# Residual tails and the products behind them, each made in two halves of 256 tokens

## The reference

```python
for l in range(2):
    f = swiglu(modulate(x, sh1, sc1), ffn_in[l, 0], ffn_out[l, 0])        # 1024 -> 2 x 2816 -> 1024
    x = deepnorm_residual(x, f, g1, ln_g[l, 0], ln_b[l, 0], 0.5)
    u = modulate(x, sh2, sc2)
    m = even_mixer(u, ...) if l % 2 == 0 else odd_mixer(u, ...)
    x = deepnorm_residual(x, m, g2, ln_g[l, 1], ln_b[l, 1])
    f = swiglu(modulate(x, sh3, sc3), ffn_in[l, 1], ffn_out[l, 1])
    x = deepnorm_residual(x, f, g3, ln_g[l, 2], ln_b[l, 2], 0.5)

def deepnorm_residual(x, f, gate, g, b, weight=1.0):
    return layer_norm(DN_ALPHA * x + weight * (1 + gate) * f, g, b)
```

## Time and profile before

| | |
|---|---|
| median of 3 runs | 4384.92 us (4381.69 to 4387.60) |
| the profiled execution | 4387.7 us, span 4386.4 us |
| PE busy | 4034.4 us, 92% |
| DVE, ACT, POOL busy | 2238.6, 1410.3, 1089.6 us |
| granted PE clock, mean | 0.946 |
| chain that ended last | 80% PE, 13% DVE |

### The profile page before, as it was taken

One profiled execution on the slowest core, in us unless ns is written; L12 is line 12 of the kernel. 1 busy time (PEld: TensorE's weight loads), 2 busy tenths in 40 slices (PEclk: granted clock), 3 DMA queues, 4 the chain that ended last, 5 costly groups with the idle time before them and its releaser, 6 DMA issues.

```text
span 4386.4 us, 48161 instructions
## 1 busy us (share of the span) xinstructions
PE 4034.4 (92%) x18728; PEld 3124.4 (71%) x18728; DVE 2238.6 (51%) x3628; ACT 1410.3 (32%) x2392; POOL 1089.6 (25%) x689
## 2 busy tenths in 40 slices
PE   5998768889998999898999899989999989999999
PEld 4886556758885887466886775778868867668777
DVE  5555772576677433544334888421363358630452
ACT  3222432432222222333232223433254232343352
POOL 1112433231012101112001329123202332424214
PEclk9999889989999999898999897999999989999899
DMA  7564133236553332102232110011101211113203
GB/s 253 175 195 152 58 107 122 92 112 189 179 173 123 103 106 85 50 27 74 92 100 72 53 44 26 28 44 58 53 15 32 65 48 54 39 41 89 63 18 94
DMA packets 115441, 384.49 MB, mean 88 GB/s; under 512 B 12688, under 2 KB 12688, under 8 KB 114576
## 3 DMA queue, kind: packets, MB, share of 16 engines
q1 hardware_dynamic: 114784, 378.80, 27.2%
q10 hardware_dynamic: 432, 2.62, 0.2%
HBM read 379.27 MB, written 2.10 MB: 87 GB/s over the span
## 4 chain that ended last, share of the span: by engine, by line
PE 80%; DVE 13%; ACT 2%; issue 2%; POOL 1%; DMA 1%; SPq 0%; DVEq 0%; ACTq 0%; POOLq 0%
PE ps L507 20%; PE ps L508 20%; PE ps L509 20%; PE ps L1372 5%; PE ps L1391 4%; DVE cut L1668 3%; PE ps L1381 2%; PE ps L772 1%; DVE cut L819 1%; PE ps L531 1%; PE ps L1601 1%; PE ps L532 1%; PE ps L533 1%; DVE cut L913 1%; PE ps L505 1%
## 5 line engine op out<-in xcount | busy, mean ns | idle before, releaser
L507 PE MATMUL ps<-cut 128*128 128x512 f32 (+1 forms) x4480 | 1731.1, 386 | 196.7 <-POOL cut L843 53.0
L508 PE MATMUL ps<-cut 128*128 128x512 f32 (+1 forms) x4480 | 1704.4, 380 | 0.0
L509 PE MATMUL ps<-cut 128*128 128x512 f32 (+1 forms) x4480 | 1701.5, 380 | 0.0
L507 PEld LDWEIGHTS ps<-cut 128*128 128x128 f32 x4480 | 859.3, 192 | 413.5 <-issue 129.5
L508 PEld LDWEIGHTS ps<-cut 128*128 128x128 f32 x4480 | 862.1, 192 | 156.5 <-issue 6.6
L509 PEld LDWEIGHTS ps<-cut 128*128 128x128 f32 x4480 | 860.5, 192 | 158.7
L443 POOL TENSOR_TENSOR cut<-cut 128x1024 fp32r<-128x1024 f32 (+1 forms) x244 | 539.8, 2216 | 1325.0 <-ACT cut L433 1324.8
L433 ACT ACTIVATE cut<-cut 128x1024 fp32r<-128x1024 f32 (+3 forms) x568 | 528.9, 944 | 691.4 <-PE ps L509 659.4
L443 DVE TENSOR_TENSOR cut<-cut 128x1024 fp32r<-128x1024 f32 (+1 forms) x324 | 411.6, 1285 | 271.1 <-ACT cut L433 268.5
L733 POOL TENSOR_TENSOR cut<-cut 128x512 fp32r<-128x512 f32 x88 | 132.5, 1505 | 1072.4 <-ACT cut L695 1072.4
L1668 DVE SCALAR_TENSOR_TENSOR cut<-cut,cols 128x512 f32<-128x512 f32 (+1 forms) x330 | 280.8, 851 | 11.7
(11 more groups left out here) (253 smaller groups left out, 3733.4 us busy)
## 6 DMA issues: line engine op xcount, KB each, us to landing
cut<-in_ffn_in SPq DMA_DIRECT2D x176, 512.0 KB, 4.1
cut<-in_mod_w SPq DMA_DIRECT2D x128, 512.0 KB, 4.0
cut<-in_ffn_out SPq DMA_DIRECT2D x64, 384.0 KB, 3.3
cut<-in_w_ada SPq DMA_DIRECT2D x48, 512.0 KB, 3.7
cut<-in_w_merge SPq DMA_DIRECT2D x48, 512.0 KB, 3.6
cut<-in_ffn_out SPq DMA_DIRECT2D x64, 320.0 KB, 3.3
cut<-in_even_in SPq DMA_DIRECT2D x32, 512.0 KB, 3.7
cut<-in_proj SPq DMA_DIRECT2D x48, 256.0 KB, 2.6
```

The source lines that it names most:

```text
L507: te.matmul(o, hi[:, k - ka, w], xs[0], start=k == 0, stop=False)
L508: te.matmul(o, hi[:, k - ka, w], xs[1], start=False, stop=False)
L509: ins = te.matmul(o, lo[:, k - ka, w], xs[0], start=False, stop=last)
```

## The change

Every tail's last product (`fo` of the second half, `ob`, `oo`) is made twice over, first for tokens 0 to 255 (A) and then for tokens 256 to 511 (B); the same weights are loaded and split for each. The layer norm of A is issued in pieces (`pe_ln`, `act_ln`, `dve_ln`, `pool_ln`) after the groups of product B: piece 0 (mean, subtraction, squares) after group 0, the sum of squares on PE after group 1, root, reciprocal and the first four tiles after group 2, and so on. The first products behind the seam are likewise made for A and then for B: 8 of the 22 groups of `gu`, the four products of tiles 0 and 1 in the recurrent branch, and all four of `oi`. The layer norm of B is issued in pieces after the groups of their A part. The low part `UL` is made half by DVE (even tiles) and half by POOL (odd tiles). Low parts of weights are made by DVE for A of a tail's product, by POOL and DVE in turn, by the slab's number, for B (`"vg"`), by POOL for A behind the seam and by DVE for B. No weight row is loaded or reduced beside a halved product. The load of the Sqrt table ahead of the tail (L776) is gone.

```diff
+def ab(*name):
+    return [name + ("A",), name + ("B",)]
+HALF = {"A": (0, 256), "B": (256, 512)}
+def ffn_parts(l, f, half):
+    whole = ("gu", l, f, half)
+    if half or (l, f) == (0, 0):
+        return [(whole, 0, (0, 512))]
+    return [(n, 0, HALF[n[-1]]) for n in ab(*whole)] + [(whole, 4, (0, 512))]
+def low_in(name):
+    return {"A": "g", "B": "v"}.get(name[-1], "v")
+def low_out(name):
+    return {"A": "v", "B": "vg"}.get(name[-1], "v")
+def low_by(n):
+    low = SLABS[n].lin.low
+    return low[n % len(low)]
-STEPS = {"xa": 0, "ga": 0, "qn": 0, "qp": 0, "kn": 0}
+def rows_in(name):
+    return 0 if name[0] in ("xa", "ga", "qn", "qp", "kn") or name[-1] in ("A", "B") else 1
...
     def pe_tail(name, x, ready, tag, nxt):
-        yield from pe_linear(name, x, ALLG, lambda m, gi: ("v_z", name, m), ready)
-        yield from pe_sum([(TOTAL, ("g_total", tag, 7))], ones, 512, ("v_cen", tag, 7), ("p_mean", tag))
-        b = bank["p_var", tag] = yield from pe_take(("a_std", tag))
-        for t in range(NT):
-            te.wait_ge(*(yield "a_sq", tag, t))
-            te.matmul(PS[b][:, :], ones, TT[t % 2], start=t == 0, stop=t == NT - 1).then_inc(*sig("p_var", tag, t))
+        for part in ab(*name):
+            after = (lambda m: pe_ln(tag, "A", m)) if part[-1] == "B" else None
+            yield from pe_linear(part, x, [HALF[part[-1]]], lambda m, gi: ("v_z", part, m),
+                                 ready if part[-1] == "A" else none, after)
+        if not nxt:
+            yield from pe_ln(tag, "B", 0)
+            yield from pe_ln(tag, "B", 1)
...
+    def pe_ln(tag, h, m):
+        g = HALF[h]
+        if m == 0:
+            yield from pe_sum([(TOTAL[:, g[0]:g[1]], ("g_total", tag, h, 7))], ones, 256, ("v_cen", tag, h, 7), ("p_mean", tag, h))
+        if m == 1:
+            b = bank["p_var", tag, h] = yield from pe_take(("a_std", tag, h))
+            for t in range(NT):
+                te.wait_ge(*(yield "a_sq", tag, h, t))
+                te.matmul(PS[b][:, 0:256], ones, sq_at(tag, h, t), start=t == 0, stop=t == NT - 1).then_inc(*sig("p_var", tag, h, t))
+    def act_ln(tag, h, m, last=4):
+        g, rstd = HALF[h], TT[2][:, HALF[h][0]:HALF[h][1]]
+        if m == 0:
+            for t in range(NT):
+                se.wait_ge(*(yield "v_cen", tag, h, t))
+                se.activation(sq_at(tag, h, t), XA[:, t, g[0]:g[1]], ACT.Square).then_inc(*sig("a_sq", tag, h, t))
+        if m == 2:
+            se.wait_ge(*(yield "p_var", tag, h, NT - 1))
+            se.activation(rstd, PS[bank["p_var", tag, h]][:, 0:256], ACT.Sqrt, ...).then_inc(*sig("a_std", tag, h))
+        if tag != "f11" and m in (3, last):
+            for t in range(4 * m - 12, 4 * m - 8 if last == 4 else NT):
+                se.wait_ge(*(yield "v_nrm", tag, h, t))
+                se.activation(UH[:, t, g[0]:g[1]], XA[:, t, g[0]:g[1]], ACT.Identity, ...).then_inc(*sig("a_uh", tag, h, t))
+    def dve_ln(tag, h, m, last=4):
...
+        if m == 0:
+            ve.wait_ge(*(yield "p_mean", tag, h))
+            for t in range(NT):
+                ve.tensor_tensor(x, x, PS[bank["p_mean", tag, h]][:, 0:256], ALU.subtract).then_inc(*sig("v_cen", tag, h, t))
+        if m == 2:
+            ve.wait_ge(*(yield "a_std", tag, h))
+            ve.reciprocal(rstd, rstd).then_inc(*sig("v_rstd", tag, h))
+        if m == 3 and tag != "f11":
+            yield from lows((0, 2))
+        for t in {2: (0, 1, 2, 3), 3: (4, 5, 6, 7)}.get(m, ()):
+            ve.tensor_tensor(x, x, rstd, ALU.mult).then_inc(*sig("v_nrm", tag, h, t))
+        for t in {2: (0, 1, 2, 3), 3: (4, 5, 6, 7)}.get(m, ()):
+            if tag == "f11":
+                ve.tensor_scalar(x, x, deriv[:, 24 + t:25 + t], deriv[:, 32 + t:33 + t], ...).then_inc(*sig("v_x", tag, h, t))
+            else:
+                if t >= 4:
+                    ve.wait_ge(*(yield ("v_ul", "g_u")[t % 2], tag, h, t - 4))
+                ve.tensor_scalar(uf(h, t), x, ca[:, t:t + 1], cbb[:, t:t + 1], ...).then_inc(*sig("v_uf", tag, h, t))
+        if m == last and tag != "f11":
+            yield from lows((4, 6))
+    def pool_ln(tag, h, m, last=4):
+        for t in ({3: (1, 3, 5, 7)} if last == 3 else {3: (1, 3), 4: (5, 7)}).get(m, ()):
+            ge.wait_ge(*(yield "a_uh", tag, h, t))
+            ge.wait_ge(*(yield "v_uf", tag, h, t))
+            ge.tensor_tensor(UL[:, t, g[0]:g[1]], uf(h, t), UH[:, t, g[0]:g[1]].bitcast(F32), ALU.subtract).then_inc(*sig("g_u", tag, h, t))
...
     def act_ffn(l, f, u, j, tag, nxt):
         for half in range(2):
-            yield from act_linear(gu, epilogue)
+            for i, (gu, tile0, g) in enumerate(ffn_parts(l, f, half)):
+                def epilogue(m):
+                    se.wait_ge(*(yield ("p_mm", gu, m) if m % 2 == 0 else ("v_hid", gu, m)))
...
+                    if gu[-1] == "A":
+                        yield from act_ln(u, "B", m)
```

More of the change, by code:

```diff
@@ L102, in weight_plan @@
     lin(("vu",), "kv_up", (), [1], kt=1, mt=8, kch=1, split=False, toks=4)
-    lin(("oo",), "odd_out", (), range(8))
+    for name in ab("oo"):
+        lin(name, "odd_out", (), range(8), low=low_out(name))
     ffn(1, 1)
@@ L438, in low_slabs @@
             to_split[which][0] += 1
-            if not SLABS[n].lin.split or SLABS[n].lin.low != which:
+            if not SLABS[n].lin.split or low_by(n) != which:
                 continue
@@ L486, in pe_weights, with pe_linear @@
         te.wait_ge(*(yield low_of(n) if SLABS[n].lin.split else raw_of(n)))
-    def pe_linear(name, x, groups, until, ready):
+    def pe_linear(name, x, groups, until, ready, after=None, beside=None):
         L = LIN[name]
@@ L790, in dve_tail, with act_tail, epilogue @@
+        if not nxt:
+            yield from pe_ln(tag, "B", 0)
+            yield from pe_ln(tag, "B", 1)
+    def act_tail(name, tag, nxt):
+        for part in ab(*name):
+            def epilogue(m):
+                if part[-1] == "B":
+                    yield from act_ln(tag, "A", m)
+            yield from act_linear(part, epilogue)
+        if not nxt:
+            for m in range(3):
+                yield from act_ln(tag, "B", m)
     def dve_tail(name, l, j, tag, nxt):
@@ new lines, in dve_tail, with pool_tail, epilogue @@
+        if not nxt:
+            for m in range(4):
+                yield from dve_ln(tag, "B", m)
+    def pool_tail(name, tag, nxt):
+        for part in ab(*name):
+            g = HALF[part[-1]]
+            def epilogue(m):
+                if m:
+                    total = TOTAL[:, g[0]:g[1]]
+                    ge.wait_ge(*(yield "v_z", part, m))
+                    if m > 1:
+                        ge.wait_ge(*(yield "g_total", tag, part[-1], m - 1))
+                    ge.tensor_tensor(total, total if m > 1 else XA[:, 0, g[0]:g[1]], XA[:, m, g[0]:g[1]],
+                                     ALU.add).then_inc(*sig("g_total", tag, part[-1], m))
+                if part[-1] == "B" and nxt:
+                    yield from pool_ln(tag, "A", m)
+            yield from pool_linear(part, epilogue)
@@ L937, in dve_rg @@
         ve.wait_ge(*prev("v"))
-        for t in range(NT + 2):
+        for t in range(2):
+            for i, kind in enumerate(("xa", "ga")):
+                yield from dve_linear((kind, t, "A"), lambda _: dve_ln(u, "B", 2 * t + i, 3))
+        for t in range(2):
+            yield from dve_linear(("xa", t, "B"), nothing)
+            yield from conv(t)
+            yield from dve_linear(("ga", t, "B"), nothing)
+            yield from dve_scale_x(u, t)
+        for t in range(2, NT + 2):
             if t < NT:
@@ L954, in part @@
             ge.tensor_tensor(YL[:, t, :], GAT[t % 4], YH[:, t, :].bitcast(F32), ALU.subtract).then_inc(*sig("g_yl", t))
-        for t in range(NT + 1):
+        for x in "AB":
+            for t in range(2):
+                for i, kind in enumerate(("xa", "ga")):
+                    yield from pool_linear((kind, t, x), lambda _: pool_ln("f00", "B", 2 * t + i, 3) if x == "A" else nothing(_))
+        for t in range(2, NT + 1):
             if t < NT:
@@ L970, in sp_rg @@
         sy.dma_start(RGW, a["rg_w"]).then_inc(*dsig("d_rg"))
-        for t in range(NT):
+        for x in "AB":
+            for t in range(2):
+                yield from sp_linear(("xa", t, x))
+                yield from sp_linear(("ga", t, x))
+        for t in range(2, NT):
             yield from sp_linear(("xa", t))
```

381 lines of the change are left out of this document (219 added, 162 removed).

## The result

The changed kernel takes 4431.48 us (median of 4 runs, 4429.19 to 4433.98) against 4386.26 (4381.69 to 4388.94) for the kernel before, measured on the same chip: ratio 1.0104, 95% interval 1.0087 to 1.0122. It is 1% slower; 0.5% faster was predicted, and the result lies outside the predicted range (4310 to 4412).

What follows compares the result with a forecast made beforehand. The prediction took PE's products in sequence as the bound; halved-product costs, waits and overlapped norms, summed by seam, gave -20.2 us: 4367.5 in the profile's terms, 4365 as a median, range 4310 to 4412.

Steps and rivals of the forecast that it cites:

- I take no change of the clock: At the seams: slow 1.2 GHz stretches counted within the old 34 us seams, and no clock change added to the sum.
- the 200 us taken off: All old seams together, from a product's last group to the later groups: 200 us removed before costs were given back.
- The waits of `fo` B: Half B of three tails beside A's norm: 13.4 us lost on late weight parts, 49.2 us in all.
- plain groups don't wait: In `f11`'s half B, 640-column parts fall on DVE; only norm pieces cost, 3.1, 4.3 and 2.4 us.
- The waits of `gu` A: `gu` half A beside B's norm: 5 us of waits from ACT's root, table loads and `UH` tiles, 32.1 us in all.
- The waits of `ob` and `oo` B: Half B of `ob` and `oo`: only the last two groups wait, 2.5 us, 29.6 us in all.
- `fo`, half A: Eight groups just fit at 31.7 us; the first waits 0.9 at `f00`, 3.0 at `f01` and `f10`.
- the rows that move to the next `fo`: Weight rows moved from the `f01` seam to the next `fo` product: +2.5 us.
- the signs that were named: If right: `fo` B about 49 us, `ob` B 30, `gu` A 32, low-part idle from under 30 to over 60.
- Rival 2: POOL's weight parts and DVE block each other in B groups and behind seams: +41 us, 4406; chance 0.28.
- Rival 3: Nothing to measure: waits a fifth larger than walked, +18 us, 4383 (4376 to 4394); chance 0.20.
- Rival 1: Overlap works better than walked, orders being kinder: half the waits gone gives 4320 us, all gone 4275; chance 0.22.

Runs made afterwards that it cites:

- e7: Changed kernel with positions loaded early and weight parts made ahead of norm pieces, POOL's running total and `gu` A's hidden tile: 4376.87 us, 0.9976 of the kernel before.
- e10: Changed kernel with early positions, A's norm behind product B, and first slab's low part on POOL, second's on DVE in all tails: 4404.05 us, 1.0039.
- e1: Changed kernel with only the positions' load issued early, before the slabs of `oi`: 4413.64 us, 1.0057 of the kernel before.
- the exchange: Edit giving `fo` B's first slab to POOL and second to DVE in `f00`, `f01`, `f10`, as in `f11`; on e7 it measured 4368.2 us.
- e9: e7 plus the exchange, the best kernel of the study: 4368.2 us, 0.9956 of the kernel before.
- e12: e9 with DVE's norm pieces in `gu` A one group later, behind the hidden tile of group 3: 4368.08 us, 0.9957 of the kernel before.

## Why the prediction was wrong

The prediction came out 66 us low in the profile's terms (4367.5 against the profiled execution's 4433.98). What it removed was right, and the waits that it walked through were nearly right. What failed were three steps: it priced every group at the full clock ("I take no change of the clock"), some 26 us; it did not see the transfer of the positions, some 15; and its waits were too short by 12, most of it in `gu` A, `ob` and `oo`. Over each stretch, the length less PE's busy time is what PE waited. Windows of `fo` B of `f00`, `f10` and `f11` in the changed kernel, of `f00` in e7, and of `f00` in e10, where nothing stands beside it (columns as above):

```profile
389.43:442.51 53.08, 38.99 (x282) 36.72 (x280) 27.71 (x45) 21.01 (x34) 24.99 (x20) 0.97 0.37 118
1728.91:1784.55 55.64, 41.88 (x282) 39.54 (x280) 28.53 (x44) 20.78 (x34) 24.99 (x20) 0.91 0.35 111
2390.26:2444.15 53.89, 42.89 (x282) 40.86 (x281) 24.87 (x41) 16.62 (x26) 20.66 (x15) 0.84 0.38 115
```
```profile
388.30:433.64 45.34, 37.46 (x282) 35.23 (x280) 29.49 (x44) 21.20 (x34) 27.61 (x19) 1.00 0.44 138
```
```profile
389.09:422.13 33.04, 33.04 (x265) 32.34 (x266) 12.75 (x17) 12.91 (x16) 19.66 (x15) 1.00 0.66 182
```

| us | waits predicted | waits measured | PE busy predicted | PE busy measured | granted clock |
|---|---|---|---|---|---|
| `fo` B, `f00` | 13.4 | 14.1 | 35.8 | 39.0 | 0.97 |
| `fo` B, `f01` | 13.4 | 13.7 | 35.8 | 40.5 | 0.94 |
| `fo` B, `f10` | 13.4 | 13.8 | 35.8 | 41.9 | 0.91 |
| `fo` B, `f11` | 9.8 | 11.0 | 35.8 | 42.9 | 0.84 |
| `ob` B, `oo` B | 2.5 each | 4.9, 4.1 | 27.1 each | 28.8 each | 0.95 |
| `gu` A of `e`, `f01`, `o` | 5.0 each | 7.0, 6.5, 6.8 | 27.1 each | 30.0, 30.3, 30.4 | 0.91 |
| all nine | 70.0 | 81.9 | 278.7 | 312.6 | |

By its own steps:

- **The clock, taken as unchanged: some +26.** PE's busy time in these nine is 34 us over the forecast. 7 of them are there at full clock too: e7 has 37.5 in `fo` B at a granted clock of 1.00 against 35.8 predicted (the bare product takes 33.0 and not 31.7). The other 26 or so go with the lower level: 1.5, 3.1, 4.4 and 5.4 in the four `fo` B, at 0.97, 0.94, 0.91 and 0.84. The step compared half B of `fo` with the recurrent gates and their 0.88, and still priced its groups at 0.120 a matmul, the full level. The old seams' slow stretches were inside the 200 us taken off, so nothing in the sum stood for the new ones. In `fo` B of `f00` the lower level came once, for 3.4 us, behind a wait of 3.47; in `f11` for 17 us in all. Not every such wait was followed by it: one of 3.08 in e7's `f00` was not. How much is also chance: `fo` B of `f01` took 54.3 in the changed kernel and 57.7 in e1, with waits of 13.7 and 13.6, and a clock of 0.94 and 0.85. No run varied the clock by itself.
- **A term that was missing: the positions' transfer, some +15.** The change moves it on SP's queue past the slabs; no step of the prediction named it. Early, it gives 15 back between the two profiled executions (18 by the medians, 21 by the ratios); put into the old kernel alone, it costs 10.
- **The waits of `fo` B: +0.7, +0.3, +0.4 and +1.2.** This walk held. At `f01` it had 0.85 a plain group, 4.0 behind the subtractions, 1.3 behind the reciprocal, 2.3 and 2.4 behind the tiles of `UL`; measured are 0.75, 3.38, 1.48, 3.47 and 3.12. In `f11` I had "plain groups don't wait", and that is right (4.1 a group; 33.3 bare); the longest wait there was 4.67, on DVE's low part (PE in the timeline of the changed kernel):

```profile
2418.70 0.58 PE L556 MATMUL ps<-cut 128*128 128x256 f32 x1 [4.67 <-DVE cut L487]
```

  The remark itself, that the slab's number decides, held the key to the other three tails and was not followed up there: on its own the exchange takes 6 us from a bare product.
- **The waits of `gu` A: 3 x 5.0 became 7.0, 6.5 and 6.8, +5.** The four `UH` tiles ahead of a high part on ACT, which the step named, are there, but ACT had before them stood 5.43 for DVE's product, behind the reciprocal and eight operations. And POOL was taken as free because 2.5 a slab is under 2.88 a group, leaving out what POOL itself waits for.
- **The waits of `ob` and `oo` B: 2 x 2.5 became 4.9 and 4.1, +4.** "Only the last two groups wait" failed: 4.13 of it in `ob` came at 961.44, on DVE's low part, 3.67 in `oo` at 2029.70, on POOL's.
- **`fo`, half A: +3.6** over four, the step being right in kind: 33.5, 36.3, 34.8 and 32.7 against 32.6, 34.7, 34.7 and 31.7.

These sum to 34 + 15 + 12 + 3.6 = 65 of the 66; as each is read from one execution, the last few us are not to be trusted. Right were: the width of 24-matmul groups (bare B products of 23.0 as predicted, and `gu` B of 23.0), the rows that move to the next `fo` (+2.4 against +2.5), and what is saved behind the last residual of `f11` (14.0 up to the program's end, against 14.3; the norm itself takes 17.6 and not 14.3, and the rest comes back behind it). Of the signs that were named, eight `fo` B groups at 49, `ob` B at 30 and `gu` A at 32 all failed by 3 to 7 us. PE's waits for low parts of weights did grow, from 69 us to 147, but the 69 were put at "under 30".

A stretch of 8 x 24 matmuls in 23.0 us is 0.120 each. By the rule of the Trainium skill ("TensorE: Matmul & The Clock Gate", the part on 56 ns against 53.3) it would be 0.109 and 21 us; the measurement is with the row of this case and not with the page.

**The rivals.** Rival 2 had the sign and the place (POOL's parts and PE waiting on them), and it named the clock as something that "would come on top", without adding it to its sum: that is the 26. Its own mechanism shows little. It had 1.0 more for each of the 24 groups of three `fo` B, and their waits were 1.4 over the walk in all; and the trace has POOL's 1024-column part at 2.36 to 2.56 us in the three `gu` A, in no case near 3, and idle time before it. Rival 3 had waits a fifth longer than walked, which is what the nine stretches have (81.9 against 70.0), but not the clock and not the positions. Reordering and the exchange, which leave every operation in, recover 1.01%, 44 us (1.0057 to 0.9956, e1 to e9). In the nine stretches PE's waits fell from 81.9 us in the changed kernel to 50.4 in e9, and its busy time, with fewer slow stretches, from 312.6 to 301.4. How much of the rest is the blocking that rival 2 meant was not measured by itself. Rival 1's argument, that orders could be kinder, is what the experiments made true by hand.

**Open.** The prediction has `e` and `o` 12 us faster each. From the start of `ob` or `oo` (its first residual less one group, 5.44 or 2.88) to the first residual of the next `fo`, `e` gained 5.2 in the changed kernel and 7.0, 5.9 and 7.5 in e7, e9 and e12, `o` 5.2 and 6.2, 6.2 and 4.3: about half of what was forecast. `gu` A keeps a stall of some 4 us that moved when its cause was moved, and `ob` and `oo` B wait 3.9 and 4.5 in e9. Whether they go with a fourth split buffer was not tried.
